# Other places in SBUF for the operands of a three-pass fp32 product stream

## What is computed

```python
# layer 0: RMSNorm -> conformer convolution module, residual; RMSNorm -> dense SwiGLU (width 2816), residual
# shared K/V: RMSNorm(x) @ w_k, @ w_v, 4 heads of 64
# layer 1: RMSNorm -> queries, chunked sliding-window attention with sinks and relative bias, w_o, residual
def swiglu(t, w_gate, w_up, w_down):
    return (jax.nn.silu(t @ w_gate) * (t @ w_up)) @ w_down
def moe_swiglu(h, router_w, router_b, w_gate, w_up, w_down):      # then: top 2 of 8 experts, width 3584
    ...
    for e in range(N_EXPERTS):
        out = out + combine[:, e:e + 1] * swiglu(t, w_gate[e], w_up[e], w_down[e])
# final RMSNorm
```

## Time and profile before

| | |
|---|---|
| median of 3 runs | 1449.49 us |
| profiled execution | 1450.4 us, its span 1448.7 us |
| TensorE (PE) matmul | 1419.3 us busy, 98% of the span, 7289 matmuls |
| TensorE weight load (PEld) | 1193.2 us |
| VectorE (DVE) | 1172.8 us, 81% |
| ScalarE (ACT) | 982.8 us, 68% |
| GpSimd (POOL) | 63.2 us |
| granted TensorE clock | 0.994 of full speed |
| DMA | 417.47 MB, 288 GB/s over the span |

### The profile page before, as it was taken

One profiled execution on the slowest core, in us unless ns is written; L12 is line 12 of the kernel. 1 busy time (PEld: TensorE's weight loads), 2 busy tenths in 40 slices (PEclk: granted clock), 3 DMA queues, 4 the chain that ended last, 5 costly groups with the idle time before them and its releaser, 6 DMA issues.

```text
span 1448.7 us, 21504 instructions
## 1 busy us (share of the span) xinstructions
PE 1419.3 (98%) x7289; PEld 1193.2 (82%) x7289; DVE 1172.8 (81%) x1321; ACT 982.8 (68%) x1197; POOL 63.2 (4%) x108
## 2 busy tenths in 40 slices
PE   8999999999899999999999999999999999999997
PEld 8886899998878888888888888888888888888885
DVE  3793354456668998999999899899989989998996
ACT  2045343445646878877887877788888778877875
POOL 1060000002220000000000000000000000000000
PEclk9999999999999999999999999999999999999998
DMA  9500665555544999999899999999999999999991
GB/s 297 202 24 21 214 197 181 195 181 172 165 130 163 380 357 343 358 360 386 317 376 368 327 367 359 353 352 363 372 329 374 360 341 365 359 376 325 373 371 76
DMA packets 194064, 417.47 MB, mean 288 GB/s; under 512 B 6912, under 2 KB 43904, under 8 KB 194015
## 3 DMA queue, kind: packets, MB, share of 16 engines
q1 hardware_dynamic: 192510, 412.79, 79.6%
q0 software_dynamic: 1344, 3.98, 1.2%
q10 hardware_dynamic: 160, 0.04, 0.0%
HBM read 414.95 MB, written 1.84 MB: 288 GB/s over the span
## 4 chain that ended last, share of the span: by engine, by line
PE 93%; DVE 2%; ACT 2%; DMA 1%; POOL 1%; issue 1%; ACTq 0%; DVEq 0%; POOLq 0%
PE bank L974 77%; PE bank L915 4%; PE bank L938 3%; PE bank L961 2%; PE bank L1225 2%; PE bank L1176 1%; PE bank L1237 1%; DVE wl L1410 1%; PE bank L870 1%; ACT wh L666 1%; POOL prob L559 1%; DMA bias<-bias_scratch 0%; PE bank L882 0%; ACT prob L728 0%; DMA R<-in_conv_ln_b 0%
## 5 line engine op out<-in xcount | busy, mean ns | idle before, releaser
L1410 DVE TENSOR_TENSOR wl<-ring,wh 128x1024 fp32r<-128x1024 f32 x758 | 911.5, 1229 | 121.8 <-ACT wh L666 82.6
L666 ACT CAST wh<-ring 128x1024 fp32r<-128x1024 f32 x758 | 787.8, 1054 | 190.5 <-PE bank L974 190.4
L974 PE MATMUL bank<-wh,low 128*128 128x512 f32 (+1 forms) x1840 | 577.1, 393 | 3.5 <-DVE wl L1410 2.8
L974 PEld LDWEIGHTS bank<-wh,low 128*128 128x128 f32 x1840 | 339.9, 188 | 76.8 <-DVE wl L1410 8.9
L974 PE MATMUL bank<-wl,low 128*128 128x512 f32 x896 | 349.6, 390 | 0.0
L974 PE MATMUL bank<-wh,ath 128*128 128x512 f32 x528 | 206.3, 391 | 0.0
L974 PE MATMUL bank<-wh,atl 128*128 128x512 f32 x528 | 205.6, 389 | 0.0
L974 PE MATMUL bank<-wl,ath 128*128 128x512 f32 x528 | 205.5, 389 | 0.0
L974 PEld LDWEIGHTS bank<-wl,low 128*128 128x128 f32 x896 | 168.2, 188 | 36.1
L974 PEld LDWEIGHTS bank<-wl,ath 128*128 128x128 f32 x528 | 99.1, 188 | 20.8
L974 PEld LDWEIGHTS bank<-wh,ath 128*128 128x128 f32 x528 | 99.2, 188 | 20.2
(11 more groups left out here) (214 smaller groups left out, 1070.1 us busy)
## 6 DMA issues: line engine op xcount, KB each, us to landing
ring<-in_moe_w_gate SPq DMA_DIRECT2D x112, 1024.0 KB, 6.1
ring<-in_moe_w_up SPq DMA_DIRECT2D x112, 1024.0 KB, 6.2
ring<-in_moe_w_down SPq DMA_DIRECT2D x112, 1024.0 KB, 6.4
ring<-in_conv_pw_w SPq DMA_DIRECT2D x12, 1024.0 KB, 10.9
ring<-in_ffd_w_gate SPq DMA_DIRECT2D x11, 1024.0 KB, 5.3
ring<-in_ffd_w_up SPq DMA_DIRECT2D x11, 1024.0 KB, 5.3
ring<-in_ffd_w_down SPq DMA_DIRECT2D x11, 1024.0 KB, 4.9
ring<-in_w_q SPq DMA_DIRECT2D x4, 1024.0 KB, 5.0
```

Source lines behind the costliest of these rows:

```text
L666: sa.copy(wh[:, place(n, h), :], ring_half(n, h)).then_inc(wh_ready, 1)
L974: mm = pe.matmul(out_bank, lhs, rhs, start=start and n == 0, stop=stop and n == 2, **kw)
L1410: ve.tensor_tensor(wl[:, place(n, h), :], ring_half(n, h), wh[:, place(n, h), :].bitcast(F32), ALU.subtract).then_inc(wl_ready, 1)
```

## The change

The lines that allocate the buffers are put in another order. The operands named above `ath`, `atl`, `low`, `high`, `pick` and `placeT` come first, `ring` after them, and `wl` and `wh` last, behind all the small buffers.

```diff
-        ring = sb("ring", [P, RING, UNIT])
-        wh = sb("wh", [P, SPLITS, HUNIT], F32R)
-        wl = sb("wl", [P, SPLITS, HUNIT], F32R)
-        high = sb("high", [P, CHUNK + DC * S], F32R)
-        low = sb("low", [P, CHUNK + DC * S], F32R)
         ath = sb("ath", [P, 4, P], F32R)
         atl = sb("atl", [P, 4, P], F32R)
+        low = sb("low", [P, CHUNK + DC * S], F32R)
+        high = sb("high", [P, CHUNK + DC * S], F32R)
+        pick = sb("pick", [P, TT, P], F32R)
+        placeT = sb("placeT", [P, S], F32R)
+        ring = sb("ring", [P, RING, UNIT])
         hnl = sb("hnl", [P, TT, D], F32R)
         yh = sb("yh", [P, D], F32R)
         yl = sb("yl", [P, D], F32R)
-        pick = sb("pick", [P, TT, P], F32R)
-        placeT = sb("placeT", [P, S], F32R)
         gate_slot = sb("gate_slot", [P, 1])
...
         tab = sb("tab", [P, 64], I32)
+        wl = sb("wl", [P, SPLITS, HUNIT], F32R)
+        wh = sb("wh", [P, SPLITS, HUNIT], F32R)
```

## The result

The changed kernel took 1478.12 us, the median of 4 runs (1475.45 to 1481.8), against 1449.55 us of 4 runs before. The ratio is 1.0193 with a 95% interval from 1.0181 to 1.0205: **slower by 1.9%, 28.6 us**. The profiled execution took 1475.45 us, 25.0 us more than that of before.

A forecast was written before the change was run, and what follows sets the result against it. It took TensorE to bound the kernel, by the number of matmuls times the distance between their starts. 25.0 - 2.4 + 0.4 = +23.0 us on 1449.5 gave 1472.5 us, range some 1463 to 1484.

The forecast's parts named there:

- Part 1: Experts, dense down, output projection: 4368 matmuls of 512 columns take the irregular 233.0 ns, 576 being slow already; +25.0 us.
- Part 2: Dense gate, up and K: 1104 matmuls of 256 columns go from 120.0 to 117.8 ns; -2.4 us.
- Part 3: Queries: 192 matmuls become regular, 117.8 to 120.0 ns, if equal remainders by 64 decide; +0.4 us.
- Part 5: VectorE and ScalarE reading and writing the moved `wl` and `wh`: durations unchanged; 0 us.
- the distance: Reading of `qh`'s irregular period: it lies 60 KB from `wl`, where the farthest regular pair is 52 KB apart.
- The remainder reading: Reading of `qh`'s irregular period: `qh`, `ql` begin 32 bytes past a multiple of 64, their partners at a multiple.
- No change: Rival: the new pairs fall back to the regular period or something else sets `qh` apart; 1449.5 us, chance 0.18.
- price-free order of buffers: Drawn from the skill's rule of two independent TensorE read ports: no order of buffers has a price.
- Faster by the side: Rival at part 1's 4368 matmuls: stationary operands far below moving ones shorten the period; 27.5 us less, 1422 us, chance 0.32.
- Slower through VectorE: Rival: VectorE's subtraction becomes longer than 1360 ns for each half; within the 0.50 for slower.

The follow-up runs named there:

- f4: The kernel before with 192 unused bytes between `wl` and `high`; 1450.02 us in one execution.
- f3: The kernel before with 128 unused bytes between `wl` and `high`; 1471.75 us in one execution.
- f1: The changed kernel with 96 unused bytes ahead of `wl`; 1450.26 us against 1449.98 for the kernel before, ratio 0.9992.
- e2: The kernel before with 32 unused bytes ahead of `wh` and 32 behind `wl`, order and distances kept; 1469.73 us in one execution.
- e3: The kernel before with 32 unused bytes ahead of `ring`, so that every buffer moves up by 32; 1450.04 us in one execution.
- e1: The changed kernel with 32 unused bytes ahead of `wl`, so that `wl` and `wh` begin at multiples of 64; 1471.23 us, ratio 1.0146.
- f2: The kernel before with 64 unused bytes between `wl` and `high`; 1472.38 us in one execution.
- e4: The kernel before with `wh`, `wl` first, `ring` behind them and the tokens' parts last, 170 to 208 KB above the split weights; 1452.80 us in one execution.
- h1: f4 with `ath` and `atl` 64 bytes higher and `xgh`, `xgl` 192 bytes lower; 1447.70 us, ratio 0.9984 to the kernel before.
- g3: The kernel before with `ath`, `atl` 2 numbers into padded buffers, `xgh`, `xgl` 60 numbers lower, `hTh`, `hTl` 24 lower; 1461.71 us in one execution.

## Why the prediction was right, and where it was not

**The bound and the place: right.** TensorE's stream of matmuls sets the time, nothing covers a longer distance between starts, and the pairs with the split weights moving are the place. The forecast for the experts was 14.7 us for 63 matmuls and 126.6 us for a pass; measured were 14.76 and, from gather to gather in a middle pass of after, 126.6. The pass is right to the tenth by luck in part: 126.6 is 123.5 and 6.3 ns for each of its 504 matmuls, without the 72 that part 1 calls slow already, and with them it would be 126.4. The step was 7.6 ns and not 6.3, and what was slow already took that back.

```profile
946.05 0.48 PE L1176 MATMUL bank<-high,pick 128*128 128x512 f32 x1
...
1072.69 0.48 PE L1176 MATMUL bank<-high,pick 128*128 128x512 f32 x1
```

The direction came from reading four streams of the same line beside each other, of which the one with `qh` was already irregular. It held with some luck: `qh` had the offset 32, the change brought 96, and of the eight offsets in steps of 32 all but 0 and 192 give 232.4 to 234.3 ns. With 192 the same reasoning would have missed (f4: 228.9, and no loss in the total).

**Part 1, +25.0 us: right in kind, a little short.** With 234.3 in place of 233.0 ns it would be 3792 x 7.6 + 576 x 3.2 = 30.7 us, of which 28.1 in the eight passes (4032 of the 4368 matmuls). They grew by 25.1. Counted over every start of a middle pass, down grew by 7.2 ns for each and gate and up by 6.1 only, because before the change more of their starts stood above the regular period already (53 of 322, in down 6 of 160). The medians grew by 28.6.

**Part 2, -2.4 us: wrong.** Dense gate and up stayed at 120.0 ns, and the whole dense stage with K grew by 1.5 us with its down products in it. I took the irregular short period of `qh`, 117.8, for all offsets. It was measured at the offset 224, and the change brought 160, whose period is 120.0.

**Part 3, +0.4 us: wrong reason.** Equal remainders by 64 did not make `qh` and `wh` regular. The timeline of the queries after, 39 matmuls:

```profile
366.98 0.28 PE L974 MATMUL bank<-qh,wh 128*128 128x256 f32 x1
...
371.61 0.28 PE L974 MATMUL bank<-qh,wh 128*128 128x256 f32 x1
```

4.63 / 39 = 118.7 ns: the offset there is 128, which is 0 by 64 but not by 256. Nor does the offset alone give this number, since dense gate and up of f3 run at 120.0 with the same 128.

**Part 5, 0: right.** 1227 and 1051 ns.

**Which property it is.** Of the two readings the distance falls: f1 is regular at 170 to 195 KB, e2 irregular at the places of before, where the experts' pairs begin 25 to 52 KB apart. The remainder reading holds in a changed form: not each operand's remainder (e3), and not the difference by 64 (e1, f2) or 128 (f3), but by 256. It was given no preference, since both led to the same forecast.

**The rivals.** No change: excluded by the interval. The Trainium skill says in "SBUF — State Buffer", Who interferes with whom, that TensorE never waits for anyone. The price-free order of buffers that the prediction drew from it does not hold for this stream: e2 moves `wh` and `wl` by 32 bytes and costs 18.8 us. Whether TensorE waits there, and for what, no trace shows. Faster by the side: excluded by f1 and e4; both sides far apart give what their offset gives near. The chance of 0.32 for it rested on two rows that differ in side and in offset at once. Slower through VectorE: excluded by its rows.

## What to carry to other kernels

In this kernel, bound by back-to-back float32r matmuls, the SBUF order is a parameter through one number above all, the address of the stationary operand less that of the moving one, modulo 256 bytes. A 4-byte buffer in between moves what follows by 32 bytes, and 32 bytes cost 1.3% in e2, 96 bytes 1.9% in the change: where a kernel has such a bound, read the distance between starts for each pair of buffers, and if two pairs of the same form differ, pad until the large group has the best one. Test an order's effect with a pad before believing in distances.

## What was not expected of the hardware

One stream can settle into a regular period or not, at the same clock and without a wait in the profile: 226.7 or 234.3 ns for 512 columns, 113.3 to 120.0 ns for 256. The regular period isn't always the short one: at 256 columns offset 0 is the slowest of the map beside 128 and 160. The same offset gave 113.3 and 117.8, within h1 and within f4 at the same addresses, and 226.7 and 233.3 at the same place of two passes of g3. So the offset is not all: it seems to set which periods a stream can settle into, and what picks one of them is not shown; how the stream enters may count. At the offset 0 with 512 columns every run here settled at 226.7 to 226.8. What in the chip repeats every 256 bytes stays open.
